# Three places for split weights, halves made two chunks ahead before norms, and a second chunk multiplied tile by tile

## The chip, the cores and the metric

The kernel runs on one core of one Trainium2 chip. The metric is the device time of one launch in microseconds (us), median of several runs. The engines are PE (TensorE, matrix products), DVE (VectorE), ACT (ScalarE), POOL (GpSimd) and SP (SyncE, which issues the transfers).

## The reference, cut to what matters

A chain of blocks on one sequence of 512 tokens, width 1024: two "first" blocks (differential attention, pooling, convolution, MLP with squared relu, a gated embedding), then a block with latent and grouped attention and a Hyena block, each with modulation and an MLP of its own. Everything is float32. Each part begins with a norm and a product with a wide weight:

```python
def rms_norm(x, g):
    xf = x.astype(jnp.float32)
    y = xf * lax.rsqrt(jnp.mean(xf * xf, axis=-1, keepdims=True) + EPS)
    return (y * g.astype(jnp.float32)).astype(x.dtype)

for i in range(DEPTH):
    u = rms_norm(h, norm_mix_g[i])
    proj = u @ w_in[i]
    ...
    q1 = rms_norm(q[..., 0, :], q_norm_g[i])
    ...
    h = h + merged @ w_o[i]
    m = rms_norm(h, norm_mlp_g[i])
    h = h + jnp.square(jax.nn.relu(m @ w_up[i])) @ w_down[i]
    e = rms_norm(h, norm_ple_g[i])
    h = h + jax.nn.sigmoid(e @ w_ple_gate[i]) * (p[i] @ w_ple_proj[i])
```

## The kernel before, in words

**Layout.** The activations `h` are transposed: eight tiles `Hs[:, k]` of 128 channels by 512 tokens. A product in float32 is made of three matmuls on a high and a low half of either factor (`three`, L540): high by high, low by high, high by low.

**Weights.** They come as chunks of 256 output columns by 1024 rows (128x2048, 1 MB) by a DMA that SP issues into `raw`, a ring of `RAWS` = 2 places. ACT copies a chunk into its high half `wh` (`w_hi`), DVE subtracts to get the low half `wl` (`w_lo`). Both halves have rings of 2 places too; a chunk's halves wait for the sum of the chunk two before it. `w_hi(tag)` and `w_lo(tag)` split all chunks up to one behind `tag` (`ahead=1`), so that PE multiplies one chunk while the next is split. The order of instructions on each engine is the order in which the host code calls these helpers; each engine runs its list in order.

**Norms.** There are ten (n = 0 to 9). The first chunk behind a norm doesn't wait for it: `first_x` (L560) multiplies tiles that are scaled by the gain only, and the eviction multiplies by rstd. Between its tiles it puts the row sums (`square_sums`) and the product that spreads rstd over the partitions (`spread`). For n in `LATE` (1, 2, 4, 5) all chunks go that way. For n in `TWICE` (0, 3, 7, 8, 9) DVE then makes the normalized tiles (`norm`, with `rstd_h` at its start), ACT their high and DVE or POOL their low half, in place over the early ones, and from the second chunk on PE uses these. The second chunk is made by `from_x` (L553): all eight tiles for the first 128 columns, then all eight for the second 128, each of its two groups ending in one `sum`.

**Layers.** `layer(l)` (l = 0, 1; norms 0 and 3) multiplies four qk chunks, i = 0 to 3, two heads' halves each, k = 2i and 2i + 1. DVE evicts each one (`qk_x`), ACT squares it, PE sums the squares (`head_sum`, L833), DVE makes a reciprocal, ACT a root, and the head is normalized; that chain runs for all eight k. Behind qk come v, pa, cx, cc, attention and wo.

**MLPs.** `mlp(M, n)`, M = 0 to 3, has four quarters q; each has four up chunks and four down chunks. M = 0 and 1 have norms 1 and 4, and DVE has one piece of `modulation` (dot products for the later blocks' scale and shift) between the chunks c = 1 to 24. M = 2 has norm 7 and pieces of the Hyena filters (`filters`) between the chunks, M = 3 has norm 9. The tables `cs` (`("cs",)` in `loads`, L146) are loaded and split in M = 2 after the second up chunk. Norm 8 feeds `hyena`, with weights `hw`; `kv` is the context's first product, between layer 1's block and the second attention. `halves_of` is the list of chunks that are split, `plan` the list of all loads, in order; `plan[i][4]` says if an entry is split.

Of the kernel before, what the change touches and what calls it, by code (L numbers as in the profile page):

```python
# [13 lines left out]
S = 512  # L14
# [2 lines left out]
EPS = 1e-6  # L17
RAWN = 2048
RAWS = 2
NEG = -1e30  # L20
TWO_PI = 2.0 * math.pi

# [105 lines left out]
def loads():  # L128
# [12 lines left out]
    def mlp(M, l, up, down):  # L141
        for q in range(4):
            for j in range(4):
                load(("up", M, q, j), ("sum", ("up", M, q, 2 * j + 1)), piece(up, l, 0, 8, 1024 * q + 256 * j, 256))
                if M == 2 and q == 0 and j == 1:
                    load(("cs",), ("sum", ("sv", 3, 1, 3)), *[piece(n, None, 0, 4, 0, 256) for n in ("C", "S")], split="own")  # L146
            for j in range(4):
                load(("dn", M, q, j), ("sum", ("dn", M, q, 2 * j + 1)), piece(down, l, 1024 * q, 8, 256 * j, 256))

    for l in range(2):  # L150
        for i, c0 in enumerate((2048, 2304, 2560, 2816)):
# [161 lines left out]
def allocate(nc, ctx):  # L313

    _, NP = param_columns()

    def sb(name, shape, dt=F32):
        return ctx.enter_context(nc.sbuf_tensor(name, shape, dt))

    def twice(name, other, shape):  # L320

        first = nc.sbuf_tensor(name, shape, F32)
        plain = first.__enter__()
        first.__exit__(None, None, None)
# [4 lines left out]
    return dict(  # L329
        FA=FA, FB=FB, Hs=Hs, HB=HB, UH=sb("UH", [128, 8, S], FR), UL=sb("UL", [128, 8, S], FR),  # L330
        raw=sb("raw", [128, RAWS * RAWN]), wh=sb("wh", [128, RAWS * RAWN], FR),
        wl=sb("wl", [128, RAWS * RAWN], FR),
        RH=sb("RH", [128, 8, S], FR), RL=sb("RL", [128, 8, S], FR),
        SC=sb("SC", [128, 4, 528]), PB=sb("PB", [128, 2304]), PR=sb("PR", [128, NP]),
        CO=sb("CO", [128, sum(CWIDTH)]), ST=sb("ST", [128, 8, 8]), MOD=sb("MOD", [128, 2, 48, 2]),
        MC=sb("MC", [128, 32]), XS=sb("XS", [128, 32]), SH=sb("SH", [128, 8, 2], FR),
        PS=ctx.enter_context(nc.psum_tensor("PS", [128, 8 * 512], F32)))
# [20 lines left out]
def build(nc, aps, bufs, ctx, plan, offset):  # L358
# [60 lines left out]
    def pair(tag, o, n=128):  # L419
        if tag == ("cs",):  # L420
            return FB[:, CS + o:CS + o + n], FB[:, CS + 2048 + o:CS + 2048 + o + n]
        if tag == ("ct",):
            return HB[:, o:o + n], HB[:, 2048 + o:2048 + o + n]
        i = index[tag]
        a = (place[i] % RAWS) * RAWN + o
        return (wh[0:plan[i][2], a:a + n], wl[0:plan[i][2], a:a + n])

    SSQ = PB[:, 1792:2304]
# [91 lines left out]
    def tensor_program(p):  # L520
# [149 lines left out]
        def mlp(M, n):  # L670
            for q in range(4):
                for j in range(4):
                    ks, first = (2 * j, 2 * j + 1), q == 0 and j == 0
                    (first_x if first else from_x)(("up", M, q, j), [("up", M, q, k) for k in ks],
                                                   [[("r_x" if M < 2 or first else "r_sq", (M, q, k))] for k in ks], n)
# [12 lines left out]
        def layer(l):  # L688
            n = 3 * l
            for i in range(4):  # L690
                ks = (2 * i, 2 * i + 1)
                p.wait_ge("w_lo", ("qk", l, i))
                if i == 0:
                    first_x(("qk", l, 0), [("qk", l, k) for k in ks], [[("qk_x", (l, k))] for k in ks], n)
                    continue
                for m, k in enumerate(ks):
# [356 lines left out]
        def hyena():  # L1053
            low, high = range(4), range(4, 8)

            def chunk(j):
                tag = ("hw", j)
                keys = [tag + (m,) for m in range(2)]
                if j == 0:
                    first_x(tag, keys, [[("hw_x", (0, m))] for m in range(2)], 8)  # L1060
                else:
                    from_x(tag, keys, [[("hw", (j, m))] for m in range(2)], 8, of=low)

            def signal(s):
                for t4 in range(4):
# [100 lines left out]
    def scalar_program(a):  # L1166
        done = [0]
        two = Turns([0, 1])

        def w_hi(tag, ahead=1):  # L1170

            while done[0] < len(halves_of) and before(halves_of[done[0]]) <= place[index[tag]] + ahead:
# [12 lines left out]

# [109 lines left out]
        def mlp(M, n):  # L1295
            for q in range(4):
                for j in range(4):
# [26 lines left out]
                    if M < 2 and q == 0 and j == 0:  # L1324
                        for v in range(2 - M):
                            silu(M, v)
                for j in range(4):
                    w_hi(("dn", M, q, j))
                    if q == 3:
                        for k in (2 * j, 2 * j + 1):  # L1330
                            stream(n + 1, k)
                    if M == 2:
                        filters(8 * q + 4 + j)

        def layer(l):
            n = 3 * l
            w_hi(("qk", l, 0))
# [131 lines left out]
            w_hi(("up", l, 0, 0))  # L1469
            norm_root(n + 1)  # L1470
            mlp(l, n + 1)
            w_hi(("pg", l, 0))
            norm_root(n + 2)
            for k in range(2):
                a.wait_ge("ld_p", l)
# [298 lines left out]
        w_hi(("kv",))  # L1774
        context_hi()
        second_attention()
        w_hi(("up", 2, 0, 0))
        norm_root(7)
        norm_hi(7, ("up", 2, 0, 1), lambda k: MOD[:, 0, 24 + k, 0:1])
        mlp(2, 7)  # L1780
        w_hi(("hw", 0))
        norm_root(8)
        norm_hi(8, ("hw", 1), lambda k: MOD[:, 1, k, 0:1])
        hyena()
        w_hi(("up", 3, 0, 0))
        norm_root(9)
        norm_hi(9, ("up", 3, 0, 1), lambda k: MOD[:, 1, 24 + k, 0:1])
        mlp(3, 9)
# [4 lines left out]
    def vector_program(v):  # L1793
        done = [0]
        pairs = Turns([2, 3])

        def w_lo(tag, ahead=1):

            while done[0] < len(halves_of) and before(halves_of[done[0]]) <= place[index[tag]] + ahead:
# [162 lines left out]
        def mlp(M, n):  # L1962
            gate = gate_of(M)
            for q in range(4):
                for j in range(4):
# [24 lines left out]
                            v.tensor_tensor(w, w, fa(JUNK, 1024), MUL).then_inc("silu", (M, x))  # L1990
                    c = 8 * q + j
                    if M < 2 and 1 <= c <= 24:
                        modulation(M, c - 1)
                if M == 2 and q == 3:
                    gains(8)
                for j in range(4):
# [9 lines left out]
                        filters(8 * q + 4 + j)  # L2006
                    c = 8 * q + 4 + j
                    if M < 2 and 1 <= c <= 24:
                        modulation(M, c - 1)
            if M < 3:  # L2010
                early_low(n + 1, 7)

        def layer(l):
            n = 3 * l
            nlam, subg = lam[l]
            w_lo(("qk", l, 0))
            norm(n)
            if l == 0:
                for i in range(2):
# [181 lines left out]
                    if k:  # L2201
                        early_low(n + 1, k - 1)
            early_low(n + 1, 7)
            w_lo(("up", l, 0, 0))
            rstd_h(n + 1)
            mlp(l, n + 1)
            w_lo(("pg", l, 0))
            rstd_h(n + 2)
            for k in range(2):
                h, lo = proj(512 * k, 512)  # L2210
# [346 lines left out]
                w_lo(("qk", 0, 0), 0)  # L2557
        for l in range(2):
            layer(l)
        w_lo(("kv",))  # L2560
        context_low()
        gains(6)
        second_attention()
        w_lo(("up", 2, 0, 0))
        shift_sums(7)
        norm(7)
        mlp(2, 7)
        w_lo(("hw", 0))
        shift_sums(8)
        norm(8)  # L2570
        hyena()
        w_lo(("up", 3, 0, 0))
        shift_sums(9)
        norm(9)
        mlp(3, 9)
# [345 lines left out]
```

## Time and profile before

| | |
|---|---|
| median of 3 runs | 3462.68 us (3459.52 to 3463.41) |
| profiled execution | 3467.97 us, span 3466.2 us |
| granted TensorE clock, mean | 0.978 |
| PE busy | 3294.7 us |
| DVE busy | 2064.2 us |
| ACT busy | 1212.3 us |
| POOL busy | 649.7 us |
| weight chunks of 1 MB loaded | 224 |

The span goes from the first to the last instruction. A line of a timeline says when an instruction begins, how long it takes, its engine, its line, what it writes and reads with shapes, and in brackets how long the engine was idle before it and who ended that. `UH`, `UL` are high and low halves of normalized or hidden tiles in even turns, `RH`, `RL` in the others; `FA`, `FB`, `HB` large areas, `SC` scratch, `PB` the spread rstd and other parts, `ST` statistics, `PS` PSUM. One matmul of 128x128 by 128x512 follows the next after 0.23 us, though its own duration is shown as 0.39.

### The profile page before, as it was taken

To read this page: it belongs to the slowest core of one execution; us is meant where nothing else is said; L and a number is where in the kernel's file an instruction comes from. 1 tells how busy PE (TensorE), PEld (TensorE's weight loads), DVE (VectorE), ACT (ScalarE), POOL (GpSimd) and SP (SyncE) were. 2 spreads that over 40 slices of the span, in tenths; PEclk is the share of its full clock that TensorE was granted. 3 is DMA by queue.
4 is the path that set the end of the run, shared out by engine and by line. 5 is a ranking of instruction groups with operands and counts; after the bars stand their busy time and mean duration, and the time that the engine had idled before them with its cause. 6 is when DMAs were issued, how large, how long until landed. Compare 5 with 4: busy or idle time off the path is not lost.

```text
span 3466.2 us, 36823 instructions
## 1 busy us (share of the span) xinstructions
PE 3294.7 (95%) x15132; PEld 2643.2 (76%) x15132; DVE 2064.2 (60%) x2663; ACT 1212.3 (35%) x1647; POOL 649.7 (19%) x495
## 2 busy tenths in 40 slices
PE   7999999999999999999988999989999988889998
PEld 5877777888787777888876776767777767768887
DVE  6655557664765555777556556555555578954443
ACT  3233432224432343322443243333333433332222
POOL 0000000000100002999710000002333024310000
PEclk9999999999999999999999899999999989999999
DMA  2222134552222224455321000022333231222222
GB/s 103 88 85 85 63 137 182 194 182 80 93 86 81 84 73 147 169 189 189 116 79 34 17 32 13 15 89 95 116 119 130 95 117 65 73 73 97 97 97 73
DMA packets 55624, 342.97 MB, mean 99 GB/s; under 512 B 5984, under 2 KB 7328, under 8 KB 18208
## 3 DMA queue, kind: packets, MB, share of 16 engines
q1 hardware_dynamic: 54080, 337.98, 27.4%
q8 instruction: 120, 1.97, 0.2%
q10 hardware_dynamic: 1376, 2.62, 0.2%
q14 instruction: 48, 0.39, 0.0%
HBM read 328.00 MB, written 12.58 MB: 98 GB/s over the span
## 4 chain that ended last, share of the span: by engine, by line
PE 69%; DVE 14%; POOL 10%; ACT 4%; issue 2%; DMA 0%; DVEq 0%; ACTq 0%; POOLq 0%
PE PS L262 68%; POOL FA L271 9%; DVE FA L279 3%; DVE wl L271 2%; PE PS L265 1%; DVE UL L271 1%; DVE SC L279 1%; ACT wh L268 1%; DVE SC L271 1%; ACT SC L268 1%; DVE SC L288 1%; DVE FA L288 1%; DVE PB L271 1%; ACT UH L268 1%; DVE FA L271 1%
## 5 line engine op out<-in xcount | busy, mean ns | idle before, releaser
L262 PE MATMUL PS<-UH,wh 128*128 128x512 f32 x2072 | 833.8, 402 | 42.2 <-DVE wl L271 21.4
L271 DVE TENSOR_TENSOR wl<-raw,wh 128x2048 fp32r<-128x2048 f32 (+2 forms) x255 | 562.3, 2205 | 443.1 <-ACT wh L268 443.0
L262 PE MATMUL PS<-UH,wl 128*128 128x512 f32 x2072 | 813.1, 392 | 0.0
L262 PE MATMUL PS<-UL,wh 128*128 128x512 f32 x2072 | 812.8, 392 | 0.0
L262 PE MATMUL PS<-RH,wh 128*128 128x512 f32 (+2 forms) x1688 | 671.3, 398 | 51.0 <-DVE RL L279 16.6
L262 PE MATMUL PS<-RL,wh 128*128 128x512 f32 (+2 forms) x1688 | 659.9, 391 | 0.0
L262 PE MATMUL PS<-RH,wl 128*128 128x512 f32 (+2 forms) x1688 | 659.3, 391 | 0.0
L268 ACT ACTIVATE wh<-raw 128x2048 fp32r<-128x2048 f32 (+2 forms) x255 | 454.5, 1783 | 320.1 <-PE PS L262 317.6
L262 PEld LDWEIGHTS PS<-UH,wh 128*128 128x128 f32 x2072 | 392.8, 190 | 160.3 <-issue 27.3
L262 PEld LDWEIGHTS PS<-UL,wh 128*128 128x128 f32 x2072 | 393.2, 190 | 84.3 <-issue 6.3
L262 PEld LDWEIGHTS PS<-UH,wl 128*128 128x128 f32 x2072 | 392.5, 189 | 83.6
L262 PEld LDWEIGHTS PS<-RH,wh 128*128 128x128 f32 (+1 forms) x1688 | 321.6, 191 | 134.7 <-DVE wl L271 32.7
L271 POOL TENSOR_TENSOR PB<-PB,SC 128x512 f32<-128x512 f32 x96 | 164.8, 1717 | 1368.5 <-ACT SC L268 1343.0
L271 POOL TENSOR_TENSOR FA<-FA 128x256 f32<-128x256 f32 (+3 forms) x298 | 350.9, 1178 | 299.0 <-PE PS L262 204.1
L262 PEld LDWEIGHTS PS<-RH,wl 128*128 128x128 f32 (+1 forms) x1688 | 321.7, 191 | 67.2
L262 PEld LDWEIGHTS PS<-RL,wh 128*128 128x128 f32 (+1 forms) x1688 | 322.0, 191 | 65.3 <-issue 1.9
L262 PE MATMUL PS<-FA 128*64 128x128 f32 (+6 forms) x1152 | 219.1, 351 | 1.7 <-ACT PB L268 1.7
L268 ACT ACTIVATE SC<-PS 128x512 f32<-128x512 f32 (+3 forms) x146 | 81.7, 560 | 347.6 <-PE PS L262 281.6
L262 PEld LDWEIGHTS PS<-FA 128*64 128x64 f32 (+2 forms) x1152 | 136.8, 153 | 62.8 <-issue 59.0
L268 ACT ACTIVATE PB<-PS,ST 128x768 f32<-128x768 f32 (+4 forms) x128 | 91.5, 715 | 234.3 <-DVE ST L275 234.1
L268 ACT ACTIVATE SC<-SC 128x512 f32<-128x512 f32 x104 | 65.6, 632 | 293.8 <-DVE SC L279 227.6
L279 DVE SCALAR_TENSOR_TENSOR FA<-FA 128x1024 f32<-128x1024 f32 (+2 forms) x124 | 161.8, 1305 | 7.6
(191 smaller groups left out, 3278.7 us busy)
## 6 DMA issues: line engine op xcount, KB each, us to landing
raw<-in_wall SPq DMA_DIRECT2D x224, 1024.0 KB, 4.8
FA<-in_wmod SPq DMA_DIRECT2D x48, 1024.0 KB, 4.9
raw<-in_wall SPq DMA_DIRECT2D x29, 512.0 KB, 3.5
kspec<-FA SPq DMA_DIRECT2D x8, 1024.0 KB, 7.1
FA<-kspec SPq DMA_DIRECT2D x8, 1024.0 KB, 4.8
PB<-in_window SPq DMA_DIRECT2D x16, 256.0 KB, 4.5
raw<-in_wall SPq DMA_DIRECT2D x8, 272.0 KB, 2.7
Hs<-in_xT ACTq DMA_DIRECT2D x4, 512.0 KB, 10.4
```

The lines of the kernel that those rows point to most:

```text
L262: return self.put(self.eng and self.eng.matmul(out, w, x, start=start, stop=stop, skip_group_check=True))
L265: return self.put(self.eng and self.eng.transpose(out, in_, ident))
L268: return self.put(self.eng and self.eng.activation(out, in_, func, **kw))
L271: return self.put(self.eng and self.eng.tensor_tensor(out, a, b, op))
L279: return self.put(self.eng and self.eng.scalar_tensor_tensor(out=out, in0=a, scalar=s, in1=b, op0=op0, op1=op1, **kw))
L288: return self.put(self.eng and self.eng.reciprocal(out, in_))
```

## The change

What it does:
- `PLACES` = 3: the rings of `wh` and `wl` have three places; `raw` keeps two. To make the room, the DMA scratch of the program is set to 1024 (no DMA of POOL is in it).
- In front of the norms and row sums, and of the context, `w_hi` and `w_lo` split two chunks ahead: qk(l,0), up(l,0,0), pg(l,0), kv, up(2,0,0), hw 0, up(3,0,0). In the MLPs 0 and 1 they do so too, for chunks c = 1 to 24: DVE behind the evictions of a chunk and in front of its modulation, ACT behind the squares. Elsewhere it stays one ahead. `blocked` keeps them from running past a plan entry that isn't split.
- The second chunk of the norms in `TWICE` is multiplied tile by tile: six matmuls per tile, both sums end with tile 7. In the layers `head_sum(l, 0)` comes after tile 4 and `head_sum(l, 1)` after tile 6 of it, `head_sum(l, 2)` and the one of k − 1 after the first group of the third chunk.
- `cs` is loaded and split behind the first down chunk of M = 2.

```diff
 RAWS = 2
+PLACES = 3
...
-                if M == 2 and q == 0 and j == 1:
-                    load(("cs",), ("sum", ("sv", 3, 1, 3)), ..., split="own")
             for j in range(4):
                 load(("dn", M, q, j), ...)
+                if M == 2 and q == 0 and j == 0:
+                    load(("cs",), ("sum", ("sv", 3, 1, 3)), ..., split="own")
...
-        def from_x(tag, keys, frees, n, of=range(8)):
+        def from_x(tag, keys, frees, n, of=range(8), by_tile=False, between=None):
             p.wait_ge("w_lo", tag)
+            if by_tile:
+                for key, fr in zip(keys, frees):
+                    take(key, *fr, of=of)
+                for k in range(8):
+                    for e in x_made(n, k):
+                        p.wait_ge(*e)
+                    for m, key in enumerate(keys):
+                        three(ps(key), pair(tag, 256 * k + 128 * m), X(n, k), k == 0, k == 7)
+                        if k == 7:
+                            p.then_inc("sum", key)
+                    if between is not None:
+                        between(k)
+                return
...
+                    if first:
+                        first_x(tag, keys, frees, n)
+                    else:
+                        from_x(tag, keys, frees, n, by_tile=n in TWICE and q == 0 and j == 1)
...
+                if i == 1:
+                    from_x(("qk", l, 1), [...], [...], n, by_tile=True,
+                           between=lambda t: head_sum(l, t // 2 - 2) if t in (4, 6) else None)
+                    continue
...
-                    if i == 1 and m == 0:
-                        head_sum(l, 0)
+                    if i == 2 and m == 0:
+                        head_sum(l, 2)
                     head_sum(l, k - 1)
...
+        def blocked(tag):
+            return any(plan[x][4] is False for x in range(index[tag] + 1, halves_of[done[0]] - 1))
         def w_hi(tag, ahead=1):
-            while done[0] < len(halves_of) and before(...) <= place[index[tag]] + ahead:
+            while done[0] < len(halves_of) and before(...) <= place[index[tag]] + ahead and not blocked(tag):
...
-                elif place[i] >= RAWS:
-                    a.wait_ge(*plan[ring[place[i] - RAWS]][5])
+                elif place[i] >= PLACES:
+                    a.wait_ge(*plan[ring[place[i] - PLACES]][5])
...  (mlp, ACT)
+                    if M < 2 and 1 <= 8 * q + j <= 24:
+                        w_hi(("up", M, q, j), 2)
...  (mlp, DVE)
                     if M < 2 and 1 <= c <= 24:
+                        w_lo(("up", M, q, j), 2)
                         modulation(M, c - 1)
...
-            w_lo(("qk", l, 0))
+            w_lo(("qk", l, 0), 2)
             norm(n)
```

## Rows read from the trace of the kernel before

**Rows 1.** The page, busy time, share of the span and instructions of each engine.
```profile
PE 3294.7 (95%) x15132; PEld 2643.2 (76%) x15132; DVE 2064.2 (60%) x2663; ACT 1212.3 (35%) x1647; POOL 649.7 (19%) x495
```
**Rows 2.** PE's waits: waited for, us in total, times, longest us.
```profile
PE PS L262 <- DVE UL L271: 36.4, 21, 6.3
PE PS L262 <- DVE wl L271: 35.9, 18, 6.7
```
**Rows 3.** Timeline of DVE at norm 0: start, us, engine, what, idle before.
```profile
35.63 2.29 DVE L271 TENSOR_TENSOR wl<-raw,wh 128x2048 fp32r<-128x2048 f32 x1 [2.84 <-ACT wh L268]
37.84 0.15 DVE L276 TENSOR_SCALAR ST<-PS 128x4 f32<-128x4 f32 x1
...
54.54 1.29 DVE L271 TENSOR_TENSOR FA<-PS,PB 128x512 f32<-128x512 f32 x2
...
57.94 0.68 DVE L282 COPY FA<-PS 128x512 f32<-128x512 f32 x1
```
**Rows 4.** Timelines at norm 3: PE at one tile, DVE's COPY, PE at chain's end.
```profile
926.69 0.50 PE L262 MATMUL PS<-UH,wh 128*128 128x512 f32 x1 [0.96 <-DVE UL L271]
...
936.49 0.68 DVE L282 COPY FA<-PS 128x512 f32<-128x512 f32 x1
...
972.83 0.67 PE L262 MATMUL PS<-SC,CO 128*128 128x512 f32 x1 [1.02 <-ACT SC L268]
```
**Rows 5.** Timelines in the first MLP: PE, DVE and ACT.
```profile
519.41 0.50 PE L262 MATMUL PS<-RH,wh 128*128 128x512 f32 x1 [2.13 <-DVE wl L271]
...
532.07 0.50 PE L262 MATMUL PS<-RH,wh 128*128 128x512 f32 x1 [1.48 <-DVE wl L271]
...
557.38 0.50 PE L262 MATMUL PS<-UH,wh 128*128 128x512 f32 x1 [0.93 <-DVE wl L271]
...
529.73 2.29 DVE L271 TENSOR_TENSOR wl<-raw,wh 128x2048 fp32r<-128x2048 f32 x1
...
536.51 1.90 ACT L268 ACTIVATE wh<-raw 128x2048 fp32r<-128x2048 f32 x1
```
**Rows 6.** Timeline of DVE in the second MLP.
```profile
1377.02 2.96 DVE L271 TENSOR_TENSOR wl<-raw,wh 128x2048 fp32r<-128x2048 f32 x1 [1.58 <-ACT wh L268]
...
1380.54 2.39 DVE L271 TENSOR_TENSOR SC<-CO,ST 128x512 f32<-128x512 f32 x1
...
1496.98 0.68 DVE L279 SCALAR_TENSOR_TENSOR SC<-PS,PB 128x512 f32<-128x512 f32 x1
...
1508.53 0.68 DVE L279 SCALAR_TENSOR_TENSOR SC<-PS,PB 128x512 f32<-128x512 f32 x1
...
1513.24 0.69 DVE L271 TENSOR_TENSOR UL<-SC,UH 128x512 fp32r<-128x512 f32 x1 [1.36 <-ACT UH L268]
```
**Rows 7.** Timelines at the context's product: DVE and PE.
```profile
1795.30 2.29 DVE L271 TENSOR_TENSOR wl<-raw,wh 128x2048 fp32r<-128x2048 f32 x1 [2.50 <-ACT wh L268]
...
1798.13 0.55 PE L262 MATMUL PS<-RH,wh 128*128 128x256 f32 x1 [6.86 <-DVE RL L279]
```
**Rows 8.** Timeline of PE behind norm 7, at two chunks.
```profile
2321.42 0.80 PE L262 MATMUL PS<-RH,wh 128*128 128x512 f32 x1 [4.44 <-DVE wl L271]
...
2361.15 0.50 PE L262 MATMUL PS<-UH,wh 128*128 128x512 f32 x1 [2.55 <-DVE wl L271]
```
**Rows 9.** Timelines behind norm 8: PE at two chunks, DVE between.
```profile
2772.39 0.80 PE L262 MATMUL PS<-RH,wh 128*128 128x512 f32 x1 [3.62 <-DVE wl L271]
...
2788.19 2.29 DVE L271 TENSOR_TENSOR HB<-raw,HB 128x2048 fp32r<-128x2048 f32 x1 [0.26 <-ACT HB L268]
...
2793.43 0.77 PE L262 MATMUL PS<-RH,wh 128*128 128x512 f32 x1 [6.28 <-DVE UL L271]
```
**Rows 10.** Timeline of PE behind norm 9, third chunk.
```profile
3120.84 0.80 PE L262 MATMUL PS<-UH,wh 128*128 128x512 f32 x1 [2.71 <-DVE wl L271]
```
**Rows 11.** Windows: us, busy of PE, PEld, DVE, ACT, POOL, PEclk, DMA share, GB/s.
```profile
2309.00:2313.00 4.00, 3.59 (x16) 2.91 (x17) 2.51 (x5) 1.54 (x3) 0.00 (x0) 1.00 0.02 4
3120.00:3127.00 7.00, 6.17 (x15) 4.81 (x16) 4.50 (x6) 3.55 (x4) 0.00 (x0) 0.51 0.41 150
```

More of the change, by code:

```diff
@@ L144, in mlp @@
                 load(("up", M, q, j), ("sum", ("up", M, q, 2 * j + 1)), piece(up, l, 0, 8, 1024 * q + 256 * j, 256))
-                if M == 2 and q == 0 and j == 1:
-                    load(("cs",), ("sum", ("sv", 3, 1, 3)), *[piece(n, None, 0, 4, 0, 256) for n in ("C", "S")], split="own")
             for j in range(4):
                 load(("dn", M, q, j), ("sum", ("dn", M, q, 2 * j + 1)), piece(down, l, 1024 * q, 8, 256 * j, 256))
+                if M == 2 and q == 0 and j == 0:
+                    load(("cs",), ("sum", ("sv", 3, 1, 3)), *[piece(n, None, 0, 4, 0, 256) for n in ("C", "S")], split="own")
     for l in range(2):
@@ L330, in allocate @@
         FA=FA, FB=FB, Hs=Hs, HB=HB, UH=sb("UH", [128, 8, S], FR), UL=sb("UL", [128, 8, S], FR),
-        raw=sb("raw", [128, RAWS * RAWN]), wh=sb("wh", [128, RAWS * RAWN], FR),
-        wl=sb("wl", [128, RAWS * RAWN], FR),
+        raw=sb("raw", [128, RAWS * RAWN]), wh=sb("wh", [128, PLACES * RAWN], FR),
+        wl=sb("wl", [128, PLACES * RAWN], FR),
         RH=sb("RH", [128, 8, S], FR), RL=sb("RL", [128, 8, S], FR),
@@ L424, in pair @@
         i = index[tag]
-        a = (place[i] % RAWS) * RAWN + o
+        a = (place[i] % PLACES) * RAWN + o
         return (wh[0:plan[i][2], a:a + n], wl[0:plan[i][2], a:a + n])
@@ L673, in mlp @@
                     ks, first = (2 * j, 2 * j + 1), q == 0 and j == 0
-                    (first_x if first else from_x)(("up", M, q, j), [("up", M, q, k) for k in ks],
-                                                   [[("r_x" if M < 2 or first else "r_sq", (M, q, k))] for k in ks], n)
+                    tag, keys = ("up", M, q, j), [("up", M, q, k) for k in ks]
+                    frees = [[("r_x" if M < 2 or first else "r_sq", (M, q, k))] for k in ks]
+                    if first:
+                        first_x(tag, keys, frees, n)
+                    else:
+                        from_x(tag, keys, frees, n, by_tile=n in TWICE and q == 0 and j == 1)
                     if M == 2:
@@ L695, in layer @@
                     continue
+                if i == 1:
+                    from_x(("qk", l, 1), [("qk", l, k) for k in ks], [[("qk_x", (l, k))] for k in ks], n, by_tile=True,
+                           between=lambda t: head_sum(l, t // 2 - 2) if t in (4, 6) else None)
+                    continue
                 for m, k in enumerate(ks):
@@ L1061, in chunk @@
                 else:
-                    from_x(tag, keys, [[("hw", (j, m))] for m in range(2)], 8, of=low)
+                    from_x(tag, keys, [[("hw", (j, m))] for m in range(2)], 8, of=low, by_tile=j == 1)
             def signal(s):
@@ L1168, in scalar_program @@
         two = Turns([0, 1])
+        def blocked(tag):
+            return any(plan[x][4] is False for x in range(index[tag] + 1, halves_of[done[0]] - 1))
         def w_hi(tag, ahead=1):
-            while done[0] < len(halves_of) and before(halves_of[done[0]]) <= place[index[tag]] + ahead:
+            while done[0] < len(halves_of) and before(halves_of[done[0]]) <= place[index[tag]] + ahead and not blocked(tag):
                 i = halves_of[done[0]]
@@ L1331, in mlp @@
                             stream(n + 1, k)
+                    if M < 2 and 8 * q + 4 + j <= 24:
+                        w_hi(("dn", M, q, j), 2)
                     if M == 2:
@@ L1336, in layer @@
             n = 3 * l
-            w_hi(("qk", l, 0))
+            w_hi(("qk", l, 0), 2)
             norm_root(n)
@@ L1468, in layer @@
                     stream(n + 1, k)
-            w_hi(("up", l, 0, 0))
+            w_hi(("up", l, 0, 0), 2)
             norm_root(n + 1)
             mlp(l, n + 1)
-            w_hi(("pg", l, 0))
+            w_hi(("pg", l, 0), 2)
             norm_root(n + 2)
@@ L1773, in scalar_program @@
             layer(l)
-        w_hi(("kv",))
+        w_hi(("kv",), 2)
         context_hi()
         second_attention()
-        w_hi(("up", 2, 0, 0))
+        w_hi(("up", 2, 0, 0), 2)
         norm_root(7)
@@ L1780, in scalar_program @@
         mlp(2, 7)
-        w_hi(("hw", 0))
+        w_hi(("hw", 0), 2)
         norm_root(8)
@@ L1784, in scalar_program @@
         hyena()
-        w_hi(("up", 3, 0, 0))
+        w_hi(("up", 3, 0, 0), 2)
         norm_root(9)
@@ L1795, in vector_program, with blocked @@
         pairs = Turns([2, 3])
+        def blocked(tag):
+            return any(plan[x][4] is False for x in range(index[tag] + 1, halves_of[done[0]] - 1))
         def w_lo(tag, ahead=1):
-            while done[0] < len(halves_of) and before(halves_of[done[0]]) <= place[index[tag]] + ahead:
+            while done[0] < len(halves_of) and before(halves_of[done[0]]) <= place[index[tag]] + ahead and not blocked(tag):
                 i = halves_of[done[0]]
@@ L2203, in layer @@
             early_low(n + 1, 7)
-            w_lo(("up", l, 0, 0))
+            w_lo(("up", l, 0, 0), 2)
             rstd_h(n + 1)
             mlp(l, n + 1)
-            w_lo(("pg", l, 0))
+            w_lo(("pg", l, 0), 2)
             rstd_h(n + 2)
@@ L2559, in vector_program @@
             layer(l)
-        w_lo(("kv",))
+        w_lo(("kv",), 2)
         context_low()
@@ L2567, in vector_program @@
         mlp(2, 7)
-        w_lo(("hw", 0))
+        w_lo(("hw", 0), 2)
         shift_sums(8)
@@ L2571, in vector_program @@
         hyena()
-        w_lo(("up", 3, 0, 0))
+        w_lo(("up", 3, 0, 0), 2)
         shift_sums(9)
```

5 lines of the change are left out of this document (3 added, 2 removed).

## The prediction

> **What bounds the kernel now.** I read the page's totals first: PE is busy 95% of the span [rows 1], so about 171 us of the 3466.2 are left to win and any other microsecond lives on an engine that makes PE wait. The table of PE's waits then says on whom: DVE subtractions, `UL` and `wl` first, 36.4 and 35.9 us [rows 2]. One `wl` wait of 6.7 is at the very start, where no ring helps; 29 us remain for a third place, if DVE has the time. Then I went through the timelines of PE and DVE at each norm and in the two MLPs with modulation, because those are the places that the diff names, and asked at each: which DVE instruction releases PE next, and what now stands in front of it. A `wl` subtraction is 2.29 us of DVE, its `wh` 1.90 us of ACT [rows 3, 5]; the change deletes none of them, it only moves them. So every gain is a `wl` taken out of a stall and every loss is the same 2.2 us put in front of something that PE wants sooner.
>
> **Norms of the layers (norms 0 and 3).** Before, DVE makes one `wl` and goes straight to the rstd of the norm (35.63, then ST at 37.84 [rows 3]). After, the `wl` of the second qk chunk stands between: its raw has landed and its `wh` costs ACT 1.90, so DVE is later by 2.2 to 2.3. Nothing hides it, since the eight normalized tiles are made at DVE's pace and PE waits for them, 0.96 us at every second tile [rows 4]. The `wl` that used to stand behind the norm (two FA evictions at 54.54, `wl`, COPY at 57.94 [rows 3]) is gone there, so DVE itself would be even. But the head sums are now inside the second chunk: `head_sum(l,0)` behind tile 4 needs the first head's eviction and its square, and DVE evicts it only after its last normalized tile, at 54.54 + 2.3 = 56.8, ACT's square ends about 58.1. PE waits there with tiles 5 to 7 behind it. From 58.1 I add tiles 5 to 7 and the two sums, 5.2: sum 2 and 3 end at 63.3, and the chain of the heads, which began with COPY at 57.94, begins 5.4 later. That chain is DVE's (eviction, reciprocal and scaling of each head in turn) and PE waits at its end, in layer 1 for `ACT SC`, 1.02 us at 972.83 [rows 4]; in layer 0 likewise. So all of the delay arrives: +5.4 for norm 0. For norm 3 the same working from COPY at 936.49 [rows 4] gives stall end 937.6, sums at 942.7: +6.2. Bounds for each: 0, if the heads' chain had slack that the trace doesn't show, and 2.3 + one `wl` more, 8; I take the worked values because the wait at the chain's end is there in both layers.
>
> **First MLP (norm 1).** At 519.41, 532.07 and so on until 557.38 PE waits for `wl`: 2.13, 1.48, 1.48 (at 544.73) and 0.93, together 6.02 us in four places [rows 5]. With two ahead these are gone. What comes next: DVE's loop. Evictions from 529.73 + 2.21 to 537.3, 5.4; then it must wait for ACT's `wh`, which now has to be the one two ahead and begins after the squares (536.51, 1.90 [rows 5]), 1.1; `wl` 2.3; modulation 5.1. That is 13.9 against a PE chunk of 12.66 − 1.48 = 11.2. So DVE becomes the bound and stays it. The last hidden tile of the quarter is ready one loop and one eviction behind 531.94, at 531.94 + 12.66 + 5.4 = 550.0 now; with the first loops up to 2.1 earlier and the others longer I get 549.75. The first down product waits for it, and the second starts at 556.0 for 557.38: −1.4, not −6.0. In the second quarter the seventh tile comes 2.1 late where there was no stall: +2.1. Quarters 3 and 4: 0. Before that norm, the moved `wl` delays the rstd too, but PE comes to the spread only after tile 5 of the first chunk, later than the delayed rstd: 0, and 2.2 if PE should be there first.
>
> **Second MLP (norm 4).** Here POOL runs beside DVE: the first `wl` takes 2.96 instead of 2.29 and a 0.69 us product takes 2.39 [rows 6]. The inserted `wl` delays rstd by up to 2.4 us, the spread had no slack, and the first down product pays: +2.1 net of the small waits it removes. In its second and third quarter the DVE loop is 11.4 us (1496.98 to 1508.53 is 11.55 [rows 6]), next to PE's 10.9; the extra wait for `wh` makes it 1.1 longer. The last hidden tile's UL, 1513.24 in [rows 6] plus three chunks' lag, comes at 1517.0 where PE needs it at 1513.7 to 1513.9: +3.1, twice: +6.2. Bounds: 0 to 8.3 for the whole MLP (0 if ACT is early enough, so that the 1.1 isn't there).
> The trace shows contention with POOL as 2.96 for 2.29 and 2.39 for 0.69 [rows 3, 6]. The Trainium skill, "SBUF — State Buffer", section "Who interferes with whom", has a DVE instruction with two SBUF inputs and a GpSimd instruction lock each other out for a whole instruction; the trace agrees in kind. By that rule the inserted `wl` could lose as much as the small product did, 1.7 in place of 0.67, and the sum would be 1 higher.
>
> **kv.** Its `wl` (2.29 at 1795.30) is followed by the RL of the context, on which PE waits already 6.86 us at 1798.13 [rows 7]. A second `wl` in between is 2.2 later in full: +2.2.
>
> **Norm 7.** Tile by tile, the second chunk is through 2.0 earlier, since its second group no longer follows the last tile. The split of `cs` (one subtraction as large as that of HB, 2.29 [rows 9]) leaves this place; with `wl` already made, the third chunk starts at 2310.8 and not at 2321.42, where PE now waits 4.44 [rows 8]. From there DVE needs for each chunk evictions, a piece of the filters, their sine and halves, and a `wl`: 4.05 + 4.3 + 2.5 + 2.3 = 13.1 by its timeline, against PE's 12, so most of the 10.6 is given back; `cs` comes in front of the second down chunk, 2.29, and the chunk at 2361.15 (2.55 of wait [rows 8]) starts at 2356.95: −4.2. Bounds −10.6 (all of it kept) to 0 (all given back); the worked value lies by the end to which DVE's loop points.
>
> **Norm 8.** Second chunk ends 2764.3; the third starts there and not at 2772.39, whose 3.62 wait is for `wl` and whose next microseconds run at half clock: −8.1, and by the chunk at 2793.43 (6.28 for UL, behind HB at 2788.19 [rows 9]) it is −7.8. **Norm 9.** Third chunk at 3113.6 and not 3120.84 [rows 10] (2.71 of wait and, behind it, 6.83 us at half clock): −8.5 at the fourth chunk's end. Bounds for both together −8 to −18.
>
> **Sum.** Losses 5.4 + 6.2 + (2.1 − 1.4) + (2.1 + 6.2) + 2.2 = 22.8; gains 4.2 + 7.8 + 8.5 = 20.5: +2.3. Then the clock. The window 3120 to 3127 behind a wait of 2.71 shows 0.51, which is the lower level, 1.2 GHz; the one at 2309 to 2313, in the middle of shorter stalls, shows 1.00 [rows 10, 11]. Seven microseconds at 0.51 cost 3.4. New waits of 3 to 4 us are the two at `head_sum(l,0)`: cost between 0 and 3.4 each; I add 1.7 each, the middle, since rows of both kinds exist: +3.4. Total +5.7, that is 3473.7 for the profiled execution, which lay 5.3 over the median of the runs. So 3468.4 in the median.
> Here a rule of the skill speaks against the change: the Trainium skill, "TensorE: Matmul & The Clock Gate", section "HAM oscillation — how this bites in real kernels", has a PE that waits between bursts re-throttled each time. The row at norm 9 agrees, the one at 2309 doesn't. By it each new stall would cost and the sum would be some 3 higher.
>
> **Rivals.**
> *The stalls taken out are won, the delays are absorbed.* For it: the heads' chain is in many links and DVE is busy 60% of the span only; the two-ahead subtractions in the MLPs could be early. Against it: the waits at the chains' ends. Half of the losses: 11.4 − 20.5 = −9, and with no loss at all −20: 3454 to 3442. Chance 0.25.
> *DVE gives back the gains at norms 7 to 9.* The mechanism is one: with `wl` off the critical place PE runs into the eviction of the sums, a UL wait as the 6.28 at 2793.43; at norm 8 the raw of the fourth chunk is fetched only once the previous is split, 4.8 us of transfer later. It decides from where DVE's loop (13.1) exceeds PE's 12. Then only 10 is won: 22.8 − 10 + 3.4 = +16, 3479. Chance 0.25.
> *The change does little*: the ring's third place isn't used since `raw` keeps two places, and a load waits for the split of the chunk before; in the rows the raws have landed long before their split, so only at norm 8 is there something in it. Time within 3 us of before. Chance 0.05.
> *The balance as summed*: chance 0.45, its own range 3460 to 3477.
>
> **How the numbers follow.** 0.2% is 6.9 us, about what a measurement of this kernel can tell from no change. The forecast case lies at +5.7 with some 7 around: a tenth of it below −6.9, four tenths above +6.9. The first rival is nearly all faster, the second nearly all slower. Faster 0.25 × 0.8 + 0.05 = 0.25; slower 0.45 × 0.38 + 0.25 × 0.85 = 0.38; same the rest, 0.37. The range leaves a tenth at each end: from half of the first rival, 3452, to a little over the second, 3482.
>
> **What would show it.** Right: at norms 0 and 3 a PE wait of 3 to 4 us behind tile 4 for the square of head 0, and the chain's end wait (972.83) grown; in the first MLP `DVE wl` waits gone and `DVE UL` waits before the first down chunk in their place; at kv 6.86 grown to about 9; third chunks of norms 7, 8, 9 without `wl` wait; the `wl` total of 35.9 down to some 10. Wrong: no stall behind tile 4, or `UL` waits no larger in total than 36.4 (then about −9 or less is to be expected); or gains at norms 7 to 9 that are gone within two chunks.

## The result: 0.5% slower

| | before | changed |
|---|---|---|
| median | 3463.05 us (6 runs, 3459.52 to 3468.61) | 3483.15 us (6 runs, 3477.01 to 3488.4) |
| ratio | | 1.005, 95% interval 1.0034 to 1.0065 |
| profiled execution | 3467.97 us, span 3466.2 | 3478.29 us, span 3476.2 |
| granted clock, mean | 0.978 | 0.974 |

In a second session the ratio was 1.0049 (1.0032 to 1.0066). The forecast was 3468.4 with a range of 3452 to 3482. "Slower" had been given 0.38, hardly more than "same" with 0.37, and the forecast of +5.7 us was itself less than the 6.9 us that had been named as the least to be told from no change: the sign was right, the size about a third of what was measured. The ratio puts the kernel at 3480, inside the range by 2 us, and the median lies 1 us outside it.

The profile after answers the lines of [rows 1, 2] so. First the page's line of busy times, then PE's waits (waited for, us in total, times, longest), the largest and those that the text comes back to; the last line is of the kernel before and answers the `DVE SC` above it:

```profile
PE 3301.1 (95%) x15132; PEld 2652.2 (76%) x15132; DVE 2059.0 (59%) x2663; ACT 1211.8 (35%) x1647; POOL 645.7 (19%) x495
```
```profile
PE PS L263 <- DVE UL L272: 41.5, 18, 8.2
PE PS L263 <- DVE wl L272: 22.7, 9, 6.7
PE PS L263 <- ACT SC L269: 21.7, 15, 3.6
PE PS L263 <- DVE SC L272: 11.9, 4, 4.3
PE PS L263 <- DVE RL L280: 10.0, 3, 9.1
```
```profile
PE PS L262 <- DVE SC L271: 3.1, 2, 1.6
```

The `wl` waits fell from 35.9 us in 18 places to 22.7 in 9: what the change is for, it does, but not down to the "some 10" of the forecast. `DVE UL` grew by 5.1; `ACT SC`, which had 7.4 us in 8 places before, has 21.7 in 15: the head sums and the heads' chain behind them. `DVE SC` grew by 8.8: that is PE waiting for the rstd, in front of which the moved `wl` now stands. PE's idle time (span less busy) went from 171.5 to 175.1, +3.6, near the +2.3 that the waits were summed to before the result was known. PE's *busy* time grew by 6.4 with the same 15132 matmuls. e12 below multiplies its second chunks tile by tile too and has 3282.7, less than before, so it isn't the order of the matmuls: it is the clock.

**Stage by stage.** Both kernels issue the same number of matmuls on PE, and each stage has the same ones. So the k-th matmul's start can be compared, and the delay that a stage adds is worked out. One row for each kernel, in us; the head says from where to where the stage runs in the trace of before. Stages in between are left out (none adds more than 4.3, and those of the changed kernel sum to −1.7) but are in the whole. Where a border falls into a stretch of low clock, moving it by a few matmuls changes a number by some tenths; the one such case of more is named at e11.

```
                      start layer0  MLP0  layer1  norm4  MLP1   kv  norm7 filters norm8 norm9 | whole
from (us of before)     10     34    508    901   1367   1410  1784  2283   2380   2742  3085 |
to                      34    214    641   1093   1410   1603  1802  2380   2742   2814  3152 |
changed                4.0    8.3    2.3    9.7    5.6    5.3   2.2  -5.7   -3.2   -7.9  -8.9 |  10.0
changed, again         2.1   11.2    2.2    9.7    5.6    5.4   2.2  -5.6   -3.2   -8.0  -8.9 |   9.3
e1 late norms          1.9    1.7   -0.0   -0.2   -0.0   -0.1   0.0  -5.3    0.0   -7.7  -8.9 | -18.1
e2 layers back         1.8    1.7    2.6   -1.5    5.7    5.4   2.2  -5.6   -3.2   -8.1  -8.9 |  -7.9
e3 mlp back            6.0   12.5   -2.9    6.2    5.7   -1.9   2.2  -3.8    0.0   -9.1  -9.6 |   5.9
e5 sums behind         4.0    4.8    2.3    2.8    5.6    5.5   2.2  -3.3   -0.0   -9.2  -9.5 |   4.9
e6 qk one ahead        3.9   10.2    2.1    6.4    4.8    4.4   2.2  -5.6   -3.2   -8.1  -8.9 |   6.5
e7 kv back             4.0    8.3    2.3    9.8    5.6    5.4  -0.0  -4.7   -0.0   -9.0  -9.6 |  15.2
e8 late by groups      6.0    0.0   -0.0    0.0   -0.0   -0.0  -0.0  -3.9    0.0   -6.3  -8.4 |  -9.4
e9 cs old              2.2    1.6   -0.0   -1.5    0.0   -0.0  -0.0  -6.5   -3.2   -8.0  -9.0 | -24.3
e10 late, sums behind  2.1    4.8    0.0    2.0   -0.0   -0.0   0.0  -3.9   -0.0   -9.1  -9.6 |  -9.5
e11 up back           -0.0   12.4    5.3    9.8   -0.5    6.2   2.2  -4.1   -0.0   -7.5  -8.9 |  15.0
e12 tiles, one ahead  -0.1    0.1   -0.0   -0.1    0.0   -0.1   0.0  -5.6   -3.2   -7.8  -8.9 | -25.8
```

A stage repeats to 0.2 us where the clock is the same. The first column is no work of the change: it lies before any code that differs, and comes out between −0.1 and 6.0. It is PE's rate: from 20 to 28 us the changed kernel has 28 matmuls and the one before 50, while the granted clock reads 1.00 in both traces, so the clock's column doesn't show this part. The whole of one execution therefore moves by several microseconds, and a part worth 2 can be read in its stage and not in the total.

**The new waits, in PE's timeline** of the changed kernel, from the first layer to norm 9:

```profile
62.96 1.65 PE L263 MATMUL PS<-SC,CO 128*128 128x512 f32 x2 [2.56 <-ACT SC L269]
...
558.99 0.79 PE L263 MATMUL PS<-UH,wh 128*128 128x512 f32 x1 [3.38 <-DVE UL L272]
...
561.64 0.80 PE L263 MATMUL PS<-UH,wh 128*128 128x512 f32 x1 [1.00 <-DVE UL L272]
...
951.89 2.04 PE L263 MATMUL PS<-SC,CO 128*128 128x512 f32 x2 [3.63 <-ACT SC L269]
...
996.18 1.10 PE L263 MATMUL PS<-SC,CO 128*128 128x512 f32 x2 [2.08 <-ACT SC L269]
...
1410.24 1.22 PE L263 MATMUL PS<-SC,CO 128*128 128x512 f32 x1 [4.29 <-DVE SC L272]
...
1833.36 0.55 PE L263 MATMUL PS<-RH,wh 128*128 128x256 f32 x1 [9.06 <-DVE RL L280]
...
2362.28 0.80 PE L263 MATMUL PS<-RH,wh 128*128 128x512 f32 x1 [2.99 <-DVE wl L272]
...
2391.20 0.72 PE L263 MATMUL PS<-UH,wh 128*128 128x512 f32 x1 [3.15 <-DVE wl L272]
...
2812.42 0.77 PE L263 MATMUL PS<-RH,wh 128*128 128x512 f32 x1 [8.15 <-DVE UL L272]
```

The waits at 62.96 and 951.89 are those of `head_sum(l,0)` inside the second qk chunk. The one at 996.18 is the end of the heads' chain in layer 1 and answers the 1.02 of [rows 4]. The two at 559 and 561.6 are the first down product, waiting for the last hidden tiles. The one at 1410.24 is the spread of norm 4. 9.06 at the context answers the 6.86 of [rows 7]. At the third chunks of norms 7, 8 and 9, where before waited 4.44, 3.62 and 2.71 [rows 8 to 10], nothing stands; later ones came in their place (2362, 2391, and 8.15 for the 6.28 of [rows 9]).

### The profile page after: what moved, and what is told of

It is laid out like the page before. It is cut to its first block, busy times and chain, and to the rows that moved or that the text cites. A ratio compares the mean times of both kernels' runs of the same rounds, so it can differ in the third digit from the quotient of the medians.

```text
span 3476.2 us, 36907 instructions
## 1 busy us (share of the span) xinstructions
PE 3301.1 (95%) x15132; PEld 2652.2 (76%) x15132; DVE 2059.0 (59%) x2663; ACT 1211.8 (35%) x1647; POOL 645.7 (19%) x495
## 4 chain that ended last, share of the span: by engine, by line
PE 75%; DVE 16%; ACT 5%; issue 3%; POOL 0%; DMA 0%; DVEq 0%; ACTq 0%; POOLq 0%
PE PS L263 74%; DVE wl L272 3%; DVE FA L280 3%; DVE SC L280 2%; ACT wh L269 2%; PE PS L266 2%; ACT SC L269 1%; DVE UL L272 1%; ACT UH L269 1%; DVE SC L272 1%; DVE SC L289 1%; DVE FA L289 1%; DVE PB L272 1%; DVE FA L272 1%; ACT FA L269 1%
```

## The experiments

The edits are against the changed kernel, unless another is named. Ratios are to the kernel before, run beside each group: e1 to e4; e5, e6, e8 and e10; and, on another chip than these, e7, e9, e11 and e12. The changed kernel itself was repeated (e4) in the first group only, so where a ratio of the later groups is set against its 1.0049, that goes by way of the kernel before.

### e1: only the parts at norms 7, 8 and 9

In this and the following edits, what is shown for `w_hi` is done for `w_lo` too, and what is shown for the up chunks for the down chunks. In e1 up(l,0,0), pg(l,0) and kv go back to one ahead as qk does.

```diff
-            w_hi(("qk", l, 0), 2)
+            w_hi(("qk", l, 0))
-                        w_hi(("up", M, q, j), 2)
-                if i == 1:
-                    from_x(("qk", l, 1), ..., by_tile=True, between=...)
-                    continue
```

> Only the parts at norms 7, 8 and 9 are kept (three places, two ahead in front of them, second chunk tile by tile, cs later); layers, both first MLPs and kv are as before. Theory A (the parts add up, and the losses sit in the layers, MLPs 0 and 1 and kv): the gain of the third part stands alone, 18 to 22 us below the kernel before, about 3443. Theory B (the losses come from the third place itself, or the gains of the late norms are only a lead that something later takes back): 3458 or more.

Measured: 3449.3 us, ratio 0.9953 (0.9935 to 0.997). Theory A was right on where the gain is and is supported by the stages: −5.3, −7.7 and −8.9, all else within 2 us of zero. By the ratio it is 16 us below before, less than the 18 to 22 expected, and the median is 6 us above the 3443; the interval, 0.9935 to 0.997, holds both. So the third place itself costs nothing that can be seen, and the gains at the late norms last to the end.

### e2: layers back, and e3: MLPs back

```diff
 e2
-            w_hi(("qk", l, 0), 2)
+            w_hi(("qk", l, 0))
-                if i == 1: from_x(..., by_tile=True, between=...)
-                    if i == 2 and m == 0:
-                        head_sum(l, 2)
+                    if i == 1 and m == 0:
+                        head_sum(l, 0)
 e3
-                        w_hi(("up", M, q, j), 2)
```

> The change, with the qk part of both layers as before (one ahead in front of norms 0 and 3, the second qk chunk in two groups, head sums as before). Theory A: the two layers cost 8 and 9 us besides the scatter at the start, so some 17 us below the changed kernel, ratio to before about 1.000 (0.999 to 1.002). Theory B (the layers' delay is absorbed by the waits that follow): within 4 us of the changed kernel, ratio 1.004 or more.

> The change, without the two-ahead calls in MLPs 0 and 1 (the ones at modulation). Theory A (an ACT copy that DVE waits for lengthens its loop, so hidden tiles come late): 6 to 8 us below the changed kernel, the DVE UL waits of 3.4 and 1.0 in the first MLP gone and DVE wl waits of 2.1, 1.5, 1.5, 0.9 back. Theory B (the UL waits stand for the wl waits one for one): within 2 us of it.

Measured: e2 0.9997 (0.9983 to 1.0011), e3 1.0019 (1.0006 to 1.0033), beside 1.0049 of the changed kernel. The layers cost 0.0052, 18 us; the two-ahead calls in the MLPs 0.0030, 10 us. Theory A both times, for e3 with one detail missed. In e3 the two waits of 3.38 and 1.00 are gone and only two `wl` waits are back, 1.03 at 546.01 and 1.47 at 558.67, not the four of [rows 5]: the `wl` in front of the row sum, which e3 keeps, had already paid for the first two. That call alone makes the stage MLP 0 −2.9; the ones at modulation turn it into +2.3.

### e4: the changed kernel again

> The changed kernel itself, beside the others on the same chip. Theory A (a steady cost): ratio to before 1.003 to 1.007 again, its profile with the same waits at norms 0, 3 and 4 and low-clock stretches that lie elsewhere. Theory B (most of the distance is the clock's scatter): ratio 1.000 to 1.003 in some rounds.

Measured: 1.0049 (1.0032 to 1.0066). Theory A. The stages are the same from MLP 0 on; the start and layer 0 are 2.1 and 11.2 for 4.0 and 8.3, and it has 1.8 less between layer 0 and MLP 0. The clock of its profiled execution was 0.973.

### e5 and e6: which half of the layers' part costs

```diff
 e5
-   between=lambda t: head_sum(l, t // 2 - 2) if t in (4, 6) else None)
+   between=lambda t: (head_sum(l, 0), head_sum(l, 1)) if t == 7 else None)
 e6
-            w_hi(("qk", l, 0), 2)
+            w_hi(("qk", l, 0))
```

> The change, with head_sum(l,0) and head_sum(l,1) both behind tile 7 of the second qk chunk and not inside it; the wl in front of norms 0 and 3 stays. Theory A (the head sum inside the chunk is the larger cause: it holds tiles 5 to 7 and so the sums that start the heads' chain): no PE wait of 2.6 or 3.6 behind tile 4, the first COPY of the chain within 1 us of where before had it relative to the norm; some 6 us a layer won, 12 us below the changed kernel, ratio 1.001 to 1.003. Theory B (the wl of 2.3 in front of the rstd is the larger cause): 4 us or less won, ratio 1.004.

> The change, with one ahead in front of norms 0 and 3; the second qk chunk tile by tile with the head sums inside it stays. Theory A: only the 2.3 us of the wl come off in each layer and the wait behind tile 4 stays: 4 to 5 us below the changed kernel, ratio about 1.0035. Theory B: most of the layers' loss is gone, 14 to 17 us below, ratio 1.000.

Measured: e5 1.0012 (1.0003 to 1.0021), e6 1.0042 (1.0026 to 1.0058). e5 wins 0.0037, 13 us, and e6 0.0007, 2 us, too little to be told from nothing and less than the 4 to 5 expected. The head sum inside the chunk is the larger cause: theory A. It is seen in DVE's timeline where the chain of the heads begins in layer 1: in the changed kernel (first line) DVE, having evicted both first heads (`FA`, from 949.64), has nothing to do for 9 us, since PE holds its tiles 5 to 7 behind the head sum; in e5 (second line) the wait is 1.24.

```profile
960.09 0.69 DVE L283 COPY FA<-PS 128x512 f32<-128x512 f32 x1 [9.17 <-PE PS L263]
```
```profile
948.83 0.69 DVE L283 COPY FA<-PS 128x512 f32<-128x512 f32 x1 [1.24 <-PE PS L263]
```

In layer 0 the same COPY of the changed kernel shows it in one line; it answers the one at 57.94 in [rows 3], 8.1 later when the 4.0 of the start are taken off:

```profile
70.06 0.69 DVE L283 COPY FA<-PS 128x512 f32<-128x512 f32 x1 [7.22 <-PE PS L263]
```

### e8: late norms, second chunk in two groups

```diff
-    from_x(tag, keys, frees, n, by_tile=n in TWICE and q == 0 and j == 1)
+    from_x(tag, keys, frees, n, by_tile=False)
-    from_x(tag, keys, [...], 8, of=low, by_tile=j == 1)
+    from_x(tag, keys, [...], 8, of=low)
```

It is otherwise e1.

> The kernel with only the parts at norms 7 to 9, and there too the second chunk in two groups as before. Theory A (tile by tile is what brings the third chunk forward, since the sums no longer follow the last tile by 5 us; two ahead only takes the wl wait out): about 2/3 of the gain goes, some 6 us below the kernel before, ratio 0.998. Theory B (the wl waits of 4.4, 3.6 and 2.7 are the gain): 13 us or more below, ratio 0.996.

Measured: 0.9966 (0.9954 to 0.9979), some 12 us below before. Theory A is out, its 0.998 lying just above the interval: most of the gain is the `wl` that is ready, −3.9, −6.3 and −8.4 in the stages without any tile by tile. In e1 they are 3.3 us better in sum, which is what the pass by tiles can have added; by the intervals it is perhaps nothing.

### e10 and e12: late norms, and the layers' chunk by tiles with the sums behind it

Both keep MLPs 0 and 1 and kv as before. e10 has two ahead in front of norms 0 and 3, e12 one.

```diff
 e10, e12
-   between=lambda t: head_sum(l, t // 2 - 2) if t in (4, 6) else None)
+   between=lambda t: (head_sum(l, 0), head_sum(l, 1)) if t == 7 else None)
 e12
-            w_hi(("qk", l, 0), 2)
+            w_hi(("qk", l, 0))
```

> The parts at norms 7 to 9 together with the layers' part whose head sums stand behind tile 7 (two ahead in front of norms 0 and 3, second qk chunk tile by tile). MLPs 0 and 1 and kv are as before. Theory A: the layers' part is then worth between -3 and +2 us beside the one with late norms alone, 3441 to 3452, ratio 0.994 to 0.9965. Theory B (the wl in front of the rstd costs 2.3 in each layer and more by the clock): 5 us or more above it, ratio 0.997 or more.

> As the kernel with late norms and the head sums behind tile 7, but with one ahead in front of norms 0 and 3. Theory A (what was left of the layers' cost is the wl of 2.3 us in front of the rstd): ratio to before 0.994 to 0.9965, like the one with late norms alone. Theory B (the two sums that end together, 5 us later than the first of them did, are what is left of it): 0.998 or more.

Measured: e10 0.999 (0.998 to 0.9999), e12 0.9963 (0.9948 to 0.9978). My theory A of e10 fell, its B was right: the `wl` in front of the rstd costs in each layer (4.8 and 2.0 in its stages, of which 1.7 stands in the first stage of e1 too) and more by the clock. e12 confirms it: with that `wl` behind the norm again, the layers' stages are 0.1 and −0.1.

e12 shows one thing more. In it the pass by tiles puts PE 5.4 us ahead of before at its 144th matmul, towards the end of the second qk chunk, and nothing of that is left at the end of the layer, since the heads' chain on DVE begins where it did (57.88 for the 57.94 of [rows 3]) and PE waits for it, 2.06 at its last link:

```profile
57.88 0.69 DVE L283 COPY FA<-PS 128x512 f32<-128x512 f32 x1
```
```profile
93.95 1.10 PE L263 MATMUL PS<-SC,CO 128*128 128x512 f32 x2 [2.06 <-ACT SC L269]
```

### e9: the place of cs

It is e1 with the load of `cs` where it was, behind the second up chunk.

> The kernel with only the parts at norms 7 to 9, and the cs tables loaded and split where they were, behind the second up chunk of MLP 2. Theory A (cs stands in front of the third chunk's eviction and its split delays DVE there, as it delays it later on in the other place): the same within 2 us, ratio 0.995 to 0.996. Theory B (its place is part of the gain): 4 us or more above, ratio 0.9965 or more.

Measured: 0.9952 (0.9935 to 0.9968), as e1. Theory A: the place of `cs` is worth nothing that can be seen.

### e11 and e7: the wl in front of the row sums, and in front of the context

```diff
 e11
-            w_hi(("up", l, 0, 0), 2)
+            w_hi(("up", l, 0, 0))
 e7
-        w_hi(("kv",), 2)
+        w_hi(("kv",))
```

> The change, with one ahead in front of the row sums of norms 1 and 4. Theory A (the inserted wl runs beside POOL at norm 4, 4.62 us in the change's trace and not 2.29, and the spread waits 4.3 for it with low clock behind): 5 to 7 us below the changed kernel, ratio about 1.003. Theory B (the row sums' wait is absorbed by the first chunks of the MLP): within 2 us, ratio 1.0045 or more.

> The change, with one ahead in front of the context. Theory A: the DVE RL wait of 9.1 is 6.9 again and 2.2 us come off, ratio about 1.004. Theory B (the clock's low stretch behind it, 10.2 us, goes too): 4 us or more, ratio 1.0035 or less.

Measured: e11 1.006 (1.0046 to 1.0073), e7 1.0056 (1.0042 to 1.007). Neither is faster than the changed kernel. So of e11's theories B's number is met (0.0011 above 1.0049, 4 us, where "within 2" had been said) and A's is not, and both numbers of e7 are missed. By the stages the local mechanism is there: in e11 norm 4 costs −0.5 and not 5.6, and in e7 the wait at the context is 6.86 again. What ate it: in e11, 3.0 in MLP 0 (5.3 for 2.3), where the `wl` in front of norm 1 had been a help, and 2.1 in MLP 1 with the wait at its end, of which 0.9 lie in front of the column's border. In e7 the gain stands until 1895 us of before, where it is 2.9 us ahead of the changed kernel, and 5.4 are lost from there to 1955, in code that is the same; the granted clock over the 65 us around it is 0.74 in e7 and 0.84 in the changed kernel and in the one before. e8 and e10 lose 4 us there as well, e11 2.4, e12 and e1 nothing. The mean clock says the same (0.972 in e11 and 0.971 in e7, for 0.974 and 0.973 in the two profiles of the changed kernel). Why this stretch runs at the lower level for longer in some kernels isn't shown, nor whether it would in each execution of them; the changed kernel wasn't run on that chip, and e7 differs by the place of one pair of instructions.

## Why the prediction was right and where it was too small

**Norms 0 and 3** (forecast 5.4 and 6.2, and 1.7 each for the clock, 15.0 together). The stages say 8.3 to 11.2 and 9.7; with the layers back they are 1.7 and −1.5. The mechanism came as described. In layer 1, into which the changed kernel comes 14.4 us late, the stall ends at 951.89, which is 937.5 in the time of before, for the forecast 937.6. `COPY` begins at 960.09, which is 945.7, for the forecast 942.7: tiles 5 to 7 and the two sums took 8.2 and not 5.2. In layer 0 the stall was 2.56, under the 3 to 4 named, and `COPY` came 8.1 later than before, not 5.4. The last link's wait is 2.08 for the 1.02 of [rows 4]; its size doesn't measure the delay, since e12, whose chain is on time, has 2.06 in layer 0 where the changed kernel has 2.07.

The term mis-sized was the clock. A second one, put at nothing, was the `wl` in front of the rstd where the head sums don't stand in the way: the forecast had "DVE itself would be even", and between e10 and e12 that `wl` is 4.7 (with the 1.7 named there) and 2.1. In layer 1 the windows around the new wait show it (us, busy of PE, PEld, DVE, ACT, POOL, PEclk, DMA share, GB/s); the first two are the tiles, the third comes behind the 3.63:

```profile
936.00:944.00 8.00, 8.00 (x27) 6.11 (x28) 6.69 (x8) 2.52 (x4) 2.02 (x2) 0.79 0.40 164
944.00:951.00 7.00, 4.26 (x19) 3.18 (x17) 6.82 (x8) 2.52 (x4) 3.10 (x3) 0.99 0.00 0
951.00:958.00 7.00, 6.11 (x13) 4.18 (x14) 0.00 (x0) 1.15 (x2) 0.01 (x1) 0.52 0.00 0
```

Seven microseconds at 0.52, the lower of the two levels, cost up to 3.4 us where 1.7 had been put, and tiles 5 to 7, which start the chain, are exactly what runs in them; 8.2 for 5.2 is 3.0 of it. The same lines agree with the rule of the Trainium skill that had been set against the change, "TensorE: Matmul & The Clock Gate", section "HAM oscillation — how this bites in real kernels": work behind a wait of PE between bursts runs at the lower clock. It isn't so behind each wait of this trace: a wait for `DVE UL` in MLP 0, 1.69 at 652.67, has a granted clock of 1.00 behind it.

**MLP 0** (forecast +0.7, measured +2.3). The forecast's point was that most of what the `wl` waits cost isn't won, since DVE waits for ACT's copy instead. DVE's timeline shows that wait, 1.11 for the forecast 1.1:

```profile
548.85 2.29 DVE L272 TENSOR_TENSOR wl<-raw,wh 128x2048 fp32r<-128x2048 f32 x1 [1.11 <-ACT wh L269]
```

In the second quarter the forecast +2.1 came as +2.3. In the first quarter the second down product starts 0.1 later than before and not 1.4 earlier: the hidden tiles' wait (3.38) had been summed, the 1.00 at 561.64 and the granted clock of 0.53 from 558 to 565 hadn't. The runs also part what the forecast had summed as one: the call in front of the row sum alone is worth −2.9 (e3), the calls at modulation alone cost 5.3 (e11).

**Norm 4 and MLP 1** (forecast 2.1 + 6.2 = 8.3, measured 5.6 and 5.3: 10.9, and −1.4 in front of the norm, which e2 and e3 don't have). The norm cost more than put and the rest less. Two `wl` in a row beside POOL took 7.51 us, where [rows 6] has one in 2.96:

```profile
1399.79 7.51 DVE L272 TENSOR_TENSOR wl<-raw,wh 128x2048 fp32r<-128x2048 f32 x2 [1.57 <-ACT wh L269]
...
1402.68 4.62 DVE L272 TENSOR_TENSOR wl<-raw,wh 128x2048 fp32r<-128x2048 f32 x1
...
1400.69 4.46 POOL L272 TENSOR_TENSOR FA<-FA 128x1088 f32<-128x1088 f32 x1
```
```profile
1408.00:1415.00 7.00, 4.76 (x9) 3.15 (x10) 2.87 (x2) 0.00 (x0) 6.45 (x8) 0.52 0.64 226
```

So the second took 4.62, not the 2.4 at most that I let in, and PE waited 4.29 for the spread, with 0.52 behind it. The rule weighed there, the Trainium skill's "SBUF — State Buffer", section "Who interferes with whom", that the two engines lock each other out for whole instructions, was the better guide, and the lines agree with it: POOL's instruction ends at 1405.15, 2.47 behind the start of the `wl`, and 2.29 on top of that are 4.76 for the measured 4.62. I had put the loss by that rule at 1.7 and it was 2.3.

**kv** (2.2): 2.2.

**Norms 7, 8, 9** (−4.2, −7.8, −8.5 = −20.5): −5.7, −7.9, −8.9 = −22.5. The third chunk of norm 7 started 12.4 us earlier than before, relative to the stage's start (forecast 10.6), and the lead grew to 14.0 within it. Of these 8.3 were given back, beginning with waits of 2.42 (for `ACT PB`, at 2358.24) and 2.99 (for `wl`, at 2362.28), as DVE's loop of 13.1 against PE's 12 had said. Another −3.2 behind norm 7 wasn't in the forecast. It is the clock's: the kernel before has a granted clock of 0.53 from 2734 to 2741, the changed one 1.00 at the same place (2763 to 2771); e1, e3, e5, e7, e8, e10 and e11 don't have the gain. The reason given for norm 7's first 2.0, the pass by tiles, was less weighty than it read: e8 keeps most of all three gains without it.

**The total.** On the profiled executions the change was +10.3 (forecast +5.7). By the medians it was +20. The step that failed first is the last one, "which lay 5.3 over the median": it was true of the kernel before alone. The profiled execution of the changed kernel lay 5 *under* its median. That is 10 of the 15 us between the forecast and the median; the other 5 are the terms above. Of both the clock seems the larger part: (1 − granted clock) × span is the time that PE would save at full clock if it were busy throughout.

| execution | clock | span | (1 − clock) × span | rest |
|---|---|---|---|---|
| before, profiled | 0.978 | 3466.2 | 76 | 3390 |
| changed, profiled | 0.974 | 3476.2 | 90 | 3386 |
| changed, the slowest of its runs | 0.971 | 3486.3 | 101 | 3385 |
| changed, another | 0.972 | 3481.6 | 97 | 3384 |
| e1, profiled | 0.977 | 3448.1 | 79 | 3369 |
| e12, profiled | 0.980 | 3440.4 | 69 | 3372 |

The rest of the changed kernel is the same in all its executions and no more than that of before; its column of the clock is 14 to 25 us larger. It is a bound, since low clock while PE waits costs nothing; the 6.4 us by which PE's busy time grew is the part that is sure. The rounding of the clock alone is worth 3.5 us. In the profiled execution much of the 14 stands behind the new waits: the windows from 558, 951 and 1408 show 0.53, 0.52 and 0.52 for 7 us each, up to 3.4 apiece. Why other executions of the same kernel have 7 to 11 more (0.972, 0.971) stays open; their stages weren't recorded.

Of the rivals, the one in which DVE gives back the gains of norms 7 to 9 gave the nearest total (3479) for the wrong reason: the gains that were forecast there were kept in full. The one in which delays are absorbed was refuted by e2. So the range owes its hit to luck. The forecast case had its own range of 3460 to 3477, and both the median and the ratio lie above it; the upper end of 3482 had been set by the rival that didn't come true. What held is the mechanism, place by place; what failed is the price of a new stall, which was put at its length and half of the clock's cost, and at two of the stalls only.

## What to carry to other kernels

A larger ring lets an engine work ahead; *when* it works ahead is a second decision, and it should be put where that engine is waiting anyway, not in front of the short step that releases the next stage. Here the same call gained 3 us in front of norm 1 (e3) and 4 to 8 in front of norms 7, 8 and 9 (e8), where no wait in front of the third chunk grew by it, and cost 2 to 6 us in front of norms 0, 3 and 4 and the context, where the next step of PE was waiting for the instruction behind it. And a small product that depends on a slow chain doesn't belong in the middle of a long one on an engine that runs in order: moving two matmuls a layer from behind tiles 4 and 6 to behind tile 7 gave 13 us.

## What the runs showed that had not been expected

- A subtraction of 2.29 us took 4.62 beside POOL.
- The best kernels are e9, e1, e12 and e8, not told apart: 0.9952 (0.9935 to 0.9968), 0.9953, 0.9963 (0.9948 to 0.9978) and 0.9966. The third place with two ahead in front of norms 7 to 9 is all that it takes.
- Executions of one kernel were 11 us apart (3477.0 to 3488.4), nearly in step with a granted clock between 0.974 and 0.971; in the second session one took 3493.2 at 0.970.
- The first stage, in front of all code that differs, varied by 6 us between profiled executions although the granted clock reads 1.00 there.
